# Dividing the output product into 776 and 256 tokens instead of 648 and 384

## The reference

```
merged = sigmoid(g_a) * (y_a @ w_branch_a) + sigmoid(g_b) * (o @ w_branch_b)
h = x + merged @ w_out                  # w_out 2048 x 2048
y = h * rsqrt(mean(h*h, -1) + 1e-6) * norm_f
```

## Time and profile before

| what | us |
|---|---|
| median of three runs | 2993.76 (2991.0 to 2999.01) |
| the profiled execution | 2993.8 |
| its span in the trace | 2992.0 |
| first pass, one tile | 14.79 |
| matmuls of line 1835 over 324 columns, 3 x 512 | mean 310 to 313 ns busy each |
| the same over 384 columns, 768 | mean 337 to 343 ns busy each |

### The profile page before, as it was taken

The page is one execution under the profiler, slowest core; times in us unless marked ns, Lnnn a source line. Parts: engine busy times, 40 slices in busy tenths (PEclk is TensorE's granted clock), DMA queues, the critical chain, the costliest instruction groups (busy, mean ns, idle before and its releaser), DMA issues.

```text
span 2992.0 us, 48715 instructions
## 1 busy us (share of the span) xinstructions
PE 2937.1 (98%) x19148; PEld 2909.4 (97%) x19148; DVE 1361.5 (46%) x2579; ACT 1027.2 (34%) x1251; POOL 434.8 (15%) x1119
## 2 busy tenths in 40 slices
PE   6999999999999999999999999999999999999998
PEld 5899999999999999999999999999999999999997
DVE  6624443462444345244435524443566543422266
ACT  6235215423621541352253145225421421211242
POOL 7500330240033023003203300420000000000000
PEclk9999999999999999999999999999999999999999
DMA  6332333233233223323322332332449754332283
GB/s 184 81 106 67 85 81 99 74 84 110 64 93 83 87 72 95 100 64 93 103 80 67 88 100 65 102 101 71 149 145 300 239 186 148 104 116 74 80 246 113
DMA packets 426099, 329.05 MB, mean 110 GB/s; under 512 B 65122, under 2 KB 388274, under 8 KB 423858
## 3 DMA queue, kind: packets, MB, share of 16 engines
q1 hardware_dynamic: 425906, 326.34, 36.5%
HBM read 235.72 MB, written 73.73 MB: 103 GB/s over the span
## 4 chain that ended last, share of the span: by engine, by line
PE 76%; POOL 6%; DVE 5%; DMA 4%; SPq 4%; issue 3%; ACT 1%; POOLq 0%; DVEq 0%; ACTq 0%
PE acc L1835 69%; PE side L1978 2%; PE side L1993 2%; DMA w_raw<-in_w_branch_a 1%; SPq L517 1%; DMA work<-work 1%; PE side L1973 1%; POOL work L1291 1%; POOL work L1285 1%; DMA t_sig_ga<-work 1%; POOL work L1286 1%; PE side L1802 1%; POOL work L1288 1%; POOL work L1287 1%; POOL work L1292 1%
## 5 line engine op out<-in xcount | busy, mean ns | idle before, releaser
L1835 PE MATMUL acc<-x_high,w_high 128*128 128x344 f32 (+2 forms) x5440 | 1203.3, 324 | 5.9 <-DVE w_low L1399 2.4
L1835 PE MATMUL acc<-x_low,w_high 128*128 128x344 f32 (+2 forms) x5440 | 1178.7, 319 | 0.0
L1835 PE MATMUL acc<-x_high,w_low 128*128 128x344 f32 (+2 forms) x5440 | 1175.3, 319 | 0.0
L1835 PEld LDWEIGHTS acc<-x_low,w_high 128*128 128x128 f32 x5440 | 919.7, 188 | 0.0
L1835 PEld LDWEIGHTS acc<-x_high,w_high 128*128 128x128 f32 x5440 | 906.2, 188 | 9.9 <-DVE x_low L1414 2.2
L1835 PEld LDWEIGHTS acc<-x_high,w_low 128*128 128x128 f32 x5440 | 911.4, 188 | 0.0
L1399 DVE TENSOR_TENSOR w_low<-w_raw,w_high 128x1024 fp32r<-128x1024 f32 x233 | 286.0, 1228 | 575.3 <-ACT w_high L924 572.6
L924 ACT CAST w_high<-w_raw 128x1024 fp32r<-128x1024 f32 x232 | 242.6, 1046 | 888.7 <-PE acc L1835 797.5
L1276 POOL COPY work<-s_tables 128x28 f32 x16 | 3.3, 208 | 1476.0 <-DVE work L1552 1213.1
L1552 DVE TENSOR_TENSOR work<-work,side 128x128 f32<-128x128 f32 x64 | 18.4, 287 | 320.8 <-PE side L1978 320.8
L980 ACT ACTIVATE work<-work 128x128 f32<-128x128 f32 (+3 forms) x64 | 43.9, 686 | 160.9 <-DVE work L1560 160.7
(11 more groups left out here) (320 smaller groups left out, 2564.3 us busy)
## 6 DMA issues: line engine op xcount, KB each, us to landing
w_raw<-in_w_in SPq DMA_DIRECT2D x160, 512.0 KB, 3.9
w_raw<-in_w_out SPq DMA_DIRECT2D x48, 512.0 KB, 3.9
work<-t_sig_ga SPq DMA_DIRECT2D x24, 516.0 KB, 4.2
out<-work SPq DMA_DIRECT2D x18, 512.0 KB
t_qk<-stage SPq DMA_DIRECT2D x16, 516.0 KB, 5.1
work<-t_qk SPq DMA_DIRECT2D x16, 516.0 KB, 4.8
t_sig_gb<-stage SPq DMA_DIRECT2D x16, 516.0 KB, 4.4
t_sig_ga<-stage SPq DMA_DIRECT2D x16, 516.0 KB, 4.7
```

Source lines behind the costliest of these rows:

```text
L1835: ins = mm(acc[s][:, a, 0:n], w[b][:, kk, :], x[:, kx, c0:c0 + n], start=start, stop=stop)
```

## The change

`B1, B2 = 6, 2`: `EARLY` becomes 256 and `LATE` 388, so that the first pass has 776 columns in two blocks of 388 and six row blocks, the second 256 columns and two row blocks. The sixth row block has no room in `h` and gets a buffer of its own over `q_high` and `q_low`, which are not used any more by then. `rows_first` becomes two DMAs for each j (16 in all), the counts on `x_res` double, `add_first` has a third instruction and `turn` a sixth transpose in the first pass, the square root and the variance move from step 7 to 8, and a sixth scaling (step 19) and store (step 22) are added. At the end two row blocks are left instead of three: VectorE scales block 0 in two halves, ScalarE block 1.

```diff
--- before.py
+++ after.py
@@ -43,7 +43,7 @@
 NEG = -1e30
 WORK = 10656
 POOL_HALF = 60
-B1, B2 = 5, 3
+B1, B2 = 6, 2
 EARLY = B2 * P
 LATE = (TOK - EARLY) // 2
 DVE_A = 176
@@ -136,6 +136,7 @@
     newsum = sb("new_squares", [P, 8])
     newvar, rstd1, w1 = sb("new_variance", [P, 1]), sb("new_rstd", [P, 1]), sb("new_newton", [P, 1])
     zero1 = sb("zero1", [P, 1])
+    q_at = (nc.sbuf_base + 31) // 32 * 32
     q_high, q_low = sb("q_high", [P, TOK], F32R), sb("q_low", [P, TOK], F32R)
     k_high, k_low = sb("k_high", [P, TOK], F32R), sb("k_low", [P, TOK], F32R)
     us_diag = sb("u_new_diagonal", [P, 2, HG * NEW])
@@ -263,13 +264,17 @@
 
 
     c = Carve(work)
-    h = c.take(B1 * D_MODEL).rearrange("p (b n) -> p b n", b=B1)
+    h = c.take(5 * D_MODEL).rearrange("p (b n) -> p b n", b=5)
+    h_sixth = nc.alloc_sbuf_tensor_at("sixth_rows", [P, D_MODEL], F32, offset=q_at)
 
 
     h2 = over_xh[:, :, EARLY:EARLY + B2 * P].rearrange("p f (b n) -> p f b n", b=B2)
     h8 = over_xl[0:NEW, :, EARLY + P:EARLY + 2 * P]
     nf, junk = over_xl[:, :, EARLY:EARLY + P], over_xl[:, :, EARLY + P:EARLY + 2 * P]
-    fresh = EARLY + B2 * P
+    fresh = EARLY + 3 * P
+
+    def rows_of(b):
+        return h[:, b, :] if b < 5 else h_sixth[:, :]
     split_xl = nc.alloc_sbuf_tensor_at("split_over_x_low", [P, KT, TOK], F32R, offset=xl_at)
     raw4 = [r[:, :, :] for r in raw] + [over_xh[:, CK * n:CK * n + CK, fresh:fresh + P] for n in range(2)]
     hi4 = [b[:, :, :] for b in hi] + [split_xl[:, CK * n:CK * n + CK, fresh:fresh + P] for n in range(2)]
@@ -335,7 +340,7 @@
     BRB = BR0 + KT
     OUT0 = BR0 + 2 * KT
     HI_M = 3 * FT + 1
-    STORE = (12, 14, 16, 18, 20)
+    STORE = (12, 14, 16, 18, 20, 22)
 
     block = stack.enter_context(nc.Block())
 
@@ -765,12 +770,13 @@
 
         def rows_first(j):
             if j >= 4:
-                sp.wait_ge(x_res[j - 4], 16)
+                sp.wait_ge(x_res[j - 4], 32)
             sp.dma_start(h[:, :, j * 2 * P:(j + 1) * 2 * P],
-                         x_prompt[0, EARLY:SEQ, j * 2 * P:(j + 1) * 2 * P].rearrange("(b p) n -> p b n", p=P)).then_inc(x_res[j % 4], 16)
+                         x_prompt[0, EARLY:SEQ - P, j * 2 * P:(j + 1) * 2 * P].rearrange("(b p) n -> p b n", p=P)).then_inc(x_res[j % 4], 16)
+            sp.dma_start(h_sixth[:, j * 2 * P:(j + 1) * 2 * P], x_prompt[0, SEQ - P:SEQ, j * 2 * P:(j + 1) * 2 * P]).then_inc(x_res[j % 4], 16)
 
         def rows_last(q):
-            sp.wait_ge(x_res[q], 32)
+            sp.wait_ge(x_res[q], 64)
             for blk in range(B2):
                 sp.dma_start(h2[:, 4 * q:4 * q + 4, blk, :],
                              x_prompt[0, blk * P:(blk + 1) * P, q * 512:(q + 1) * 512].rearrange("p (f n) -> p f n", f=4)).then_inc(x_res[q], 16)
@@ -803,11 +809,11 @@
             if at in STORE:
                 blk = STORE.index(at)
                 sp.wait_ge(h_norm, blk + 1)
-                sp.dma_start(y_prompt[0, EARLY + blk * P:EARLY + (blk + 1) * P, :], h[:, blk, :]).then_inc(y_out, 16)
+                sp.dma_start(y_prompt[0, EARLY + blk * P:EARLY + (blk + 1) * P, :], rows_of(blk)).then_inc(y_out, 16)
             if at == 30:
                 sp.wait_ge(h_final, 1)
                 sp.dma_start(y_sample.rearrange("b o (f n) -> (b o) f n", f=KT), h8).then_inc(y_out, 16)
-        for blk, done, n, c0, c1 in ((0, h_final, 2, 0, WIDTH), (0, h_final, 3, WIDTH, D_MODEL), (2, h_last, 1, 0, D_MODEL), (1, h_final, 4, 0, D_MODEL)):
+        for blk, done, n, c0, c1 in ((0, h_final, 2, 0, WIDTH), (0, h_final, 3, WIDTH, D_MODEL), (1, h_last, 1, 0, D_MODEL)):
             sp.wait_ge(done, n)
             sp.dma_start(y_prompt[0, blk * P:(blk + 1) * P, c0:c1], h[:, blk, c0:c1]).then_inc(y_out, 16)
         sp.wait_ge(y_out, (B1 + 1 + B2 + 1) * 16)
@@ -1139,7 +1145,7 @@
                             act.wait_ge(o_added[s], KT // 2 + PRIMED)
                     else:
                         act.wait_ge(squared, FT + blk)
-                    nc.scalar.activation(junk, h[:, blk, :].rearrange("p (f n) -> p f n", f=KT), ACT.Square, accum_out=hvar1[:, blk:blk + 1]).then_inc(squared, 1)
+                    nc.scalar.activation(junk, rows_of(blk).rearrange("p (f n) -> p f n", f=KT), ACT.Square, accum_out=hvar1[:, blk:blk + 1]).then_inc(squared, 1)
                 if at == 2 + B1:
                     act.wait_ge(var_ready, 5)
                     nc.scalar.activation(hstd1[:, :], hvar1[:, :], ACT.Sqrt).then_inc(std_ready, 1)
@@ -1150,7 +1156,7 @@
         nc.scalar.activation(hstd2[:, :], hvar2[:, :], ACT.Sqrt).then_inc(std_ready, 1)
         act.wait_ge(h_rstd, 1)
         act.wait_ge(y_out, (B1 + 1) * 16)
-        nc.scalar.mul(h[:, 2, :].rearrange("p (f n) -> p f n", f=KT), h2[:, :, 2, :], rstd_2[:, 2:3]).then_inc(h_last, 1)
+        nc.scalar.mul(h[:, 1, :].rearrange("p (f n) -> p f n", f=KT), h2[:, :, 1, :], rstd_2[:, 1:2]).then_inc(h_last, 1)
 
 
     @block.gpsimd
@@ -1693,17 +1699,19 @@
 
         def add_first(j, s):
             dve.wait_ge(o_tr[s], j + 1 + PRIMED)
-            dve.wait_ge(x_res[j % 4], 16 * (j // 4 + 1))
+            dve.wait_ge(x_res[j % 4], 32 * (j // 4 + 1))
             f = 2 * j + s
             hs = h[:, :, f * P:(f + 1) * P]
             V.tensor_tensor(hs[:, 0:4], hs[:, 0:4], side[:, s, :].rearrange("p (b f) -> p b f", b=4), ALU.add)
-            V.tensor_tensor(hs[:, 4], hs[:, 4], acc[s][:, 2, 0:P], ALU.add).then_inc(o_added[s], 1)
+            V.tensor_tensor(hs[:, 4], hs[:, 4], acc[s][:, 2, 0:P], ALU.add)
+            h6 = h_sixth[:, f * P:(f + 1) * P]
+            V.tensor_tensor(h6, h6, acc[s][:, 2, P:2 * P], ALU.add).then_inc(o_added[s], 1)
 
         def add_last(j, s):
 
             dve.wait_ge(o_tr[s], j + (KT // 2 + 1) + PRIMED)
             f = 2 * j + s
-            dve.wait_ge(x_res[f // 4], 32 + B2 * 16)
+            dve.wait_ge(x_res[f // 4], 64 + B2 * 16)
             hs = h2[:, f]
             V.tensor_tensor(hs, hs, side[:, s, 0:EARLY].rearrange("p (b f) -> p b f", b=B2), ALU.add).then_inc(o_added[s], 1)
             dve.wait_ge(o_added[s], j + (KT // 2 + 1) + PRIMED)
@@ -1760,14 +1768,14 @@
                     if 4 * j + m < 2 * KT:
                         weigh(2 * j + m // 2 - 1)
                 at = 4 * j + m
-                if at == 7:
+                if at == 8:
                     dve.wait_ge(squared, FT + B1)
                     V.tensor_scalar(hvar1[:, :], hvar1[:, :], 1.0 / D_MODEL, EPS, ALU.mult, ALU.add).then_inc(var_ready, 1)
                     dve.wait_ge(std_ready, 5)
                     rsqrt(hvar1[:, :], hstd1[:, :], rstd_1[:, :], w4[:, :], c2)
-                if at in (9, 11, 13, 15, 17):
+                if at in (9, 11, 13, 15, 17, 19):
                     blk = (at - 9) // 2
-                    rows = h[:, blk, :].rearrange("p (f n) -> p f n", f=KT)
+                    rows = rows_of(blk).rearrange("p (f n) -> p f n", f=KT)
                     V.scalar_tensor_tensor(rows, rows, rstd_1[:, blk:blk + 1], nf, ALU.mult, ALU.mult).then_inc(h_norm, 1)
                 if at == 21:
                     new_added()
@@ -1788,7 +1796,7 @@
         rsqrt(hvar2[:, :], hstd2[:, :], rstd_2[:, :], w4[:, 0:B2], c2)
         V.tensor_copy(w4[:, 0:B2], rstd_2[:, :]).then_inc(h_rstd, 1)
         dve.wait_ge(y_out, (B1 + 1) * 16)
-        for blk, f0, f1 in ((0, 0, FT), (0, FT, KT), (1, 0, KT)):
+        for blk, f0, f1 in ((0, 0, FT), (0, FT, KT)):
             V.tensor_scalar(h[:, blk, f0 * P:f1 * P].rearrange("p (f n) -> p f n", n=P), h2[:, f0:f1, blk, :], rstd_2[:, blk:blk + 1], None, ALU.mult).then_inc(h_final, 1)
 
 
@@ -2093,7 +2101,8 @@
             for blk in range(B2 if half else 4):
                 last = tr(side[:, s, blk * P:(blk + 1) * P], stage[s][:, blk * P:(blk + 1) * P], ident[:, :])
             if half == 0:
-                last = tr(acc[s][:, 2, 0:P], stage[s][:, 4 * P:5 * P], ident[:, :])
+                for blk in range(4, B1):
+                    last = tr(acc[s][:, 2, (blk - 4) * P:(blk - 3) * P], stage[s][:, blk * P:(blk + 1) * P], ident[:, :])
             last.then_inc(o_tr[s], 1)
 
         HALF_COLS = ([(0, EARLY, LATE), (1, EARLY + LATE, LATE)], [(0, 0, EARLY)])
```

## The result

The changed kernel takes 3006.77 us (median of 7 runs, 3002.49 to 3009.99) where the kernel before took 2994.86 beside it (7 runs): a ratio of 1.0039 with a 95% interval of 1.0029 to 1.0049. It is slower, by 11.9 us in the medians, where +9.5 (3003.3) was forecast, with 2993 to 3010 as the range of 8 in 10. The time alone doesn't choose between the forecast and the rivals with some +14 (3008), since 11.9 lies between them: the trace has to. The profiled execution took 3003.05, its span is 3001.2.

What follows compares the result with a forecast made beforehand. TensorE was taken to bound the kernel, busy 98% of the span and waiting for nothing in either pass. The terms 44.3 - 45.7 + 3.1 + 3.4 + 7.4 - 3.0 gave +9.5, 3003.3 us; 8-in-10 range 2993 to 3010.

Steps and rivals of the forecast that it cites:

- rivals with some +14 (3008): Clock falling in the second pass's gap (chance 0.10), or transfers binding while row blocks are stored (0.07); each 3008 us.
- three signs: Forecast wrong if: no second-pass wait for VectorE, first-pass tile off by over 0.1 us, or clock under 1.0 before the end.
- Step 1: Matmuls of both passes: wider ones add 44.3 us in the first, narrower ones take 45.7 off the second; sum -1.4.
- The weight load: Rival, second-pass matmuls: a weight load of 188 ns binds, tiles 3.4 us longer, 3044 us; chance 0.02.
- Step 2: Beginning of the second pass: TensorE waits for chunks 5 and 6, late through loads and casts; +3.1 us.
- Step 3: Second pass, steps 2 to 17: ScalarE's list, the reciprocal and VectorE's scalings exceed 5.83 us a tile; +3.4 us.
- Step 4: Second pass, chunks 22 to 28: VectorE's list with the new rows takes 25.2 us against TensorE's 17.5; +7.4 us.
- Step 5: After the last matmul: shorter copy, fewer VectorE instructions and one 1 MB block less to store; -3.0 us.
- The waits weren't covered: Rival judged: second pass stays bound by TensorE because casts run ahead, 2989.4 us; chance 0.15.
- The transfers didn't bind: Rival judged: transfers bind while row blocks are stored, 0.75 us for six tiles, 4.5 us, 3008; chance 0.07.
- The clock did fall: Rival judged: clock falls in the 3.4 us gap ahead of chunk 25, +4.8 us at three chunks, 3008; chance 0.10.

Runs made afterwards that it cites:

- b2: Changed kernel with new rows' squares on ScalarE, norm gains and x loaded later, six tiles' second-pass squares on ScalarE too: 2995.57 us, ratio 1.0010 to the kernel before.
- c1: b2 with the square root, the reciprocal, and the six scalings and stores moved to later steps: 2994.36 us, ratio 0.9998 to the kernel before.
- a2: Changed kernel with the new rows' sixteen squares and sums made by one ScalarE instruction: 2999.72 us, ratio 1.0011 to the kernel before.
- a4: Changed kernel with the new rows' squares and sums made twice on VectorE: 3014.14 us, ratio 1.0061 to the kernel before.
- b3: Kernel before the change with the new rows' squares as one ScalarE instruction: 2995.23 us, ratio 1.0001 to the unedited kernel before.
- b4: Kernel before the change without the last scaling and store of row block 1: 2991.78 us, ratio 0.9995 to the unedited kernel before.
- a1: Changed kernel run again with no edit: 3006.33 us, ratio 1.0036 to the kernel before.

## Why the prediction was right

The direction, the mechanism and the place of each wait were forecast; the size was put at 9.5 us, and 11.9 came. All of the difference of 2.4 lies in step 1. Of the three signs by which the forecast called itself wrong, the first (TensorE doesn't wait for VectorE) didn't come; the second, a first-pass tile off by over 0.1 us, lay just at its edge (17.66 for 17.56; the pass 1.5 us longer than forecast); the third did come, a clock under 1.0 ahead of the end. What it did to the time stands under the rivals.

**Step 1** was forecast at -1.4 and gave +0.9. The number of columns does cancel, but the two distances weren't quite on the lines used: 388 columns 177.1 ns instead of 176.0, 1.7 us in the first pass (of which the table shows 1.5), and 256 columns 118 instead of 117 (a distance read between wide matmuls had to stand for a stream), 0.8 us in the second. This term is the one that was mis-sized, and its 2.3 us are nearly the whole 2.4 that the forecast is short. The formula of the Trainium skill for the isolated gap (TensorE: Matmul & The Clock Gate, section Back-to-back issue gap), columns/2.4 + 2.5 ns, gives 0.0 for this term as an estimate. That is nearer to +0.9 than the interpolation's -1.4, though each of its distances is too short by this trace: 109.2 ns for 118, 164.2 for 177.1. The weight load doesn't bind at 256 columns: b2 and c1 show it over a whole pass.

The waits of steps 2 to 4 are given by TensorE's starts: the distance from the last start of one chunk to the first of the next, less what it is where nothing is waited for (0.12 to 0.14 us).

**Step 2** (+3.1): waits of 2.3 and 1.0 us ahead of chunks 5 and 6, where they were placed; moving the loads and `weigh` took 2.7 off.

**Step 3** (+3.4): in the trace of the changed kernel 1.4 and 0.5 us ahead of chunks 11 and 12 and 0.4 each ahead of 14 and 16, 2.7 in all; b2 and c1 together, which also shorten a small wait at chunk 8, take 1.3 + 2.0 = 3.3 off. Its largest part is the root, which also held up the copy of chunk 9's tile on ScalarE, so that the transposes waited too; I had only VectorE's side of it.

**Step 4** (+7.4): 0.3, 3.4, 0.9 and 1.3 us ahead of chunks 24, 25, 26 and 28, and chunk 25 itself took 1.1 us longer, in part at half the clock: 7.0. a2 takes 6.7 off, a4 puts 7.7 on, b3 shows that the same work cost nothing at 384 columns.

Steps 2 to 4 together: sixteen undisturbed tiles of 5.90 us in place of the 8.70 of before (TensorE's starts at 2892.39 and 2901.09) would have made the second pass 142.5 - 44.8 = 97.7 us. It took 111.6, so all waits cost 13.9 us, and 13.9 were forecast. That the sum fits to a tenth is in part luck, since the steps by themselves are off by some tenths, the third by up to 0.7. The 12.9 us that the edits up to c1 took off (111.6 - 98.7) show in the windows as 9.2 us less idle time of TensorE (10.4 to 1.2) and as 3.6 us less busy time for the same 824 records (101.41 to 97.84); part of these 3.6 were matmuls at half the clock.

**Step 5** (-3.0): -3.0, and b4 separates the store's 2.4 from the rest.

**The rivals.** The waits weren't covered. The transfers didn't bind under the stores: ScalarE waited up to 2.1 us for a landing there, but VectorE behind it had no idle time from 2914.5 on until chunk 28 was cast. The weight load didn't bind either (118 ns over c1's whole pass). The clock did fall, as the rival said: after the piece of 3.4 us the window at 2966.5 has 0.50 (the 1.2 GHz level), matmuls of chunk 25 among it. But it had hardly a price where the rival put 4.8 us (for three chunks). In a1 the fall came earlier, inside the piece, and lasted twice as long,

```profile
2963.20:2970.00 6.80, 5.76 (x27) 5.80 (x28) 6.42 (x15) 1.40 (x3) 0.00 (x0) 0.50 0.26 77
```

and the second pass took the same 111.6 us. Chunk 25 now took so long that chunk 26 started 5.25 us after it without any wait, where it is 4.92 in the changed kernel; the wait ahead of chunk 28 then paid for the 0.3 us. These are its lines, first the changed kernel's, then a1's:

```profile
2977.25 0.36 PE L1843 MATMUL acc<-x_high,w_high 128*128 128x256 f32 x1 [1.13 <-DVE w_low L1748]
2976.40 0.35 PE L1843 MATMUL acc<-x_high,w_high 128*128 128x256 f32 x1 [0.62 <-DVE w_low L1748]
```

Chunk 28 starts 12.2 us after chunk 25 in both. A stretch bound by another engine hides a slower TensorE too, as long as the waits that are left are longer than what it loses. In a2 the clock fell at chunk 5 instead, and from the start of chunk 5 to that of chunk 11 it took 20.6 us where the changed kernel and a1 took 20.3: there the fall may have cost some 0.3 us.

So the change couldn't have won much even with all waits away: 404.5 - 13.9 = 390.6 us against 392.7, 2.1 less, of which c1 has 1.0. That gain is the 3.0 us of the end, less the 0.9 of step 1.

## What to carry to other kernels

When a stage bound by TensorE is shortened and others lengthened, the work of the other engines stays where its steps are written: add up each engine's list between two of TensorE's deadlines in the short stage, and don't go by its share of the span (VectorE's is 45% in the changed kernel, while two stretches are bound by it). A piece of side work (eight rows' squares in sixteen small instructions) that was free under 8.7 us tiles cost its full length under 5.9 us ones; one fused instruction on the engine that has time gave it back. Differences of a few us are to be measured from the first instruction that the change touches on, since the part ahead of it differed by 2.7 us between the two profiled executions; over all twelve traces the output product began between 2595.7 and 2604.2. And a wait is to be measured by the starts around it: the idle time in the trace was 0.2 to 0.5 us shorter at each, because the record of the last matmul or transpose runs on into the wait.

## What the runs showed of the hardware that wasn't expected

The granted clock fell to 0.5 in or behind quite short pieces without matmuls: in a2 at 2903.1, at the end of one of 2.1 us; in the changed kernel at 2966.5, 1.4 us after work had gone on behind one of 3.2; in a1 at 2963.0, inside one of 3.2; in a4 at 2966.2, inside one of 6.8. It stayed down for 3.4 us in a2 and the changed kernel, 6.8 in a1 and 10.3 in a4, where it also fell for 3.4 us twice more, at 2897.9 and 2979.9, around pieces of 2.7 and 3.0 us. In a1 and the changed kernel, after pieces of 2.1 and 2.0 us ahead of the same chunk 5, it stayed at 1.0. What decides between them is not settled by these runs.

A float32r matmul of 256 columns follows the next at 118 ns, of 384 at 174.2, of 388 at 177.1, and 384 and 392 in turn at a mean of 176.4: the step from 384 to 388 is larger than four columns at the slope from 324 to 384 (1.7 ns).
